# Sample attention in groups of four batches on the column quarters, and ScalarE's gates ahead of its state copies

## What is computed

```python
z = rmsnorm(x) @ w_in                                  # xr | gr | q | k | v | indexer ... | ga | gb
xc = causal_conv(xr)                                   # width 4
r, i = sigmoid(xc @ w_rg_a + b_a), sigmoid(xc @ w_rg_x + b_x)   # block diagonal
h[t] = a[t] * h[t-1] + sqrt(1 - a[t]**2) * i * xc      # a = exp(c * r * log_sigmoid(lam)); scan over positions
branch_a = (h * gelu(gr)) @ w_rnn_out
# sample rows: 8 batches, each with 256 past keys and values in two pages of a cache, and 4 new ones
p = softmax(mask(q @ k.T + bias)); o = p @ v           # 8 heads, mask from the indexer's top 65 keys
```

## Time and profile before

| | us |
|---|---|
| median of 3 runs | 1099.66 (1098.62 to 1100.06) |
| profiled execution, its own time | 1099.85 |
| span of the profiled execution | 1098.1 |
| PE busy | 1041.8 (95%) |
| DVE busy | 473.7 (43%) |
| ACT busy | 405.0 (37%) |
| POOL busy | 429.9 (39%) |

### The profile page before, as it was taken

The page is one execution under the profiler, slowest core; times in us unless marked ns, Lnnn a source line. Parts: engine busy times, 40 slices in busy tenths (PEclk is TensorE's granted clock), DMA queues, the critical chain, the costliest instruction groups (busy, mean ns, idle before and its releaser), DMA issues.

```text
span 1098.1 us, 19161 instructions
## 1 busy us (share of the span) xinstructions
PE 1041.8 (95%) x7847; PEld 978.8 (89%) x7847; DVE 473.7 (43%) x715; ACT 405.0 (37%) x690; POOL 429.9 (39%) x259
## 2 busy tenths in 40 slices
PE   4889999999997999999999899999999999999897
PEld 4777997777786889989999899999999999999797
DVE  2326899489988335323343413222100222212553
ACT  5424233556564434432332622222112222222534
POOL 2614432143435554534452534343444434343540
PEclk9999999999998999999999999999999999999899
DMA  6643274343312133304351332322233332222402
GB/s 180 176 78 91 60 197 133 118 116 96 96 40 77 23 80 97 97 23 124 106 164 54 103 100 85 95 67 73 87 101 106 87 95 62 61 85 81 116 1 82
DMA packets 168749, 101.96 MB, mean 93 GB/s; under 512 B 12626, under 2 KB 160754, under 8 KB 168418
## 3 DMA queue, kind: packets, MB, share of 16 engines
q1 hardware_dynamic: 168674, 100.91, 32.6%
HBM read 93.26 MB, written 7.63 MB: 92 GB/s over the span
## 4 chain that ended last, share of the span: by engine, by line
PE 81%; DVE 10%; ACT 4%; DMA 2%; issue 1%; POOL 1%; SPq 1%; DVEq 0%; ACTq 0%; POOLq 0%
PE psD L1723 71%; DVE xc L1133 3%; PE psX L1678 2%; DMA wraw<-in_w_in 1%; DVE hs L1283 1%; PE held L1678 1%; PE psX L1988 1%; PE held L1876 1%; PE held L2012 1%; DVE hs L1265 1%; DVE ig L1277 1%; PE psX L1806 1%; DVE h_lo L1063 1%; DMA prm<-in_state_rglru_h 1%; ACT L615 1%
## 5 line engine op out<-in xcount | busy, mean ns | idle before, releaser
L1509 POOL TENSOR_TENSOR wlo<-wraw,whi 128x1024 fp32r<-128x1024 f32 (+4 forms) x165 | 362.6, 2200 | 601.1 <-ACT whi L606 601.0
L1723 PE MATMUL psD<-h_hi,whi 128*128 128x272 f32 (+1 forms) x1616 | 347.8, 297 | 14.2 <-DVE h_lo L1063 9.8
L1723 PE MATMUL psD<-h_hi,wlo 128*128 128x272 f32 (+1 forms) x1616 | 338.8, 291 | 0.0
L1723 PE MATMUL psD<-h_lo,whi 128*128 128x272 f32 (+1 forms) x1616 | 338.4, 291 | 0.0
L1723 PEld LDWEIGHTS psD<-h_hi,whi 128*128 128x128 f32 (+1 forms) x1616 | 257.4, 191 | 34.8 <-issue 23.0
L1723 PEld LDWEIGHTS psD<-h_lo,whi 128*128 128x128 f32 (+1 forms) x1616 | 258.2, 191 | 0.0
L606 ACT CAST whi<-wraw 128x1024 fp32r<-128x1024 f32 (+4 forms) x165 | 154.8, 939 | 276.9 <-PE psD L1723 250.1
L1723 PEld LDWEIGHTS psD<-h_hi,wlo 128*128 128x128 f32 (+1 forms) x1616 | 256.9, 192 | 0.0
L1723 PE MATMUL psD<-act_hi,whi 128*128 128x272 f32 x672 | 140.9, 291 | 0.0
L1723 PE MATMUL psD<-act_hi,wlo 128*128 128x272 f32 x672 | 139.1, 288 | 0.0
L1723 PE MATMUL psD<-act_lo,whi 128*128 128x272 f32 x672 | 138.6, 288 | 0.0
(11 more groups left out here) (262 smaller groups left out, 942.2 us busy)
## 6 DMA issues: line engine op xcount, KB each, us to landing
wraw<-in_w_in SPq DMA_DIRECT2D x48, 512.0 KB, 4.6
wraw<-in_w_ffn_gate SPq DMA_DIRECT2D x22, 512.0 KB, 3.8
wraw<-in_w_ffn_up SPq DMA_DIRECT2D x22, 512.0 KB, 3.8
wraw<-in_w_ffn_down SPq DMA_DIRECT2D x16, 384.0 KB, 3.4
wraw<-in_w_ffn_down SPq DMA_DIRECT2D x16, 320.0 KB, 3.1
kpg<-in_cache_k SPq DMA_DIRECT2D x16, 256.0 KB, 3.0
kpg<-in_cache_v SPq DMA_DIRECT2D x16, 256.0 KB, 3.4
wraw<-in_w_rnn_out SPq DMA_DIRECT2D x8, 512.0 KB, 5.0
```

What stands on the lines that cost most here:

```text
L1509: g_.tensor_tensor(wlo[:, s, 0:rc, 0:cc], wraw[:, s, 0:rc, 0:cc], whi[:, s, 0:rc, 0:cc].bitcast(F32), ALU.subtract).then_inc(w_lo, 1)
L1723: ins = te.matmul(psD[0:cc, b0 + half, 0:HT], w[:, s, c, 0:cc], m[:, k0 + c, HT * half:HT * (half + 1)], start=(part == 0 and c == 0 and w ...
```

## The change

Four edits:
1. Past keys: four buffers `kts` in place of two. `past_logits(g4)` takes batches 4g to 4g+3 together, for each of the four contraction chunks one matmul on each column quarter in turn. PE's order: turns 0 to 3 between the halves of units 15 and 16, then logits of group 0 and turn 4 inside unit 17, turns 5 and 6, the five `vout` jobs, turn 7, logits of group 1.
2. Past values: four buffers `vpg` (the two of `kpg`, one over `kts[0]`, one over `qbd`). `past_values(g)` takes four batches together, group 0 in chunk 0 and group 1 behind gate sums (2, 1).
3. SP: value pages of batches 2 and 3 wait for both groups of logits, those of batches 4 to 7 for the first group of values; unit loads 25 and 26 come behind the first wait, 27 to 38 behind the eight page loads that follow the second.
4. ACT: in chunk c, `gates(c)` comes ahead of `final_states(c-1)`.

```diff
@@ buffers @@
+    kts = [place(f"kts{i}", [P, HP, PAST], F32, "act_lo", at) for i, at in enumerate((17920, 22016, 4096, 8192))]
+    vpg = kpg + [place("vpg2", [P, NPG, ATT], F32, "kts0"), place("vpg3", [P, NPG, ATT], F32, "qbd")]
@@ SP @@
                 job_read(sp, ("kts", NB - 2 + b, 1))
-                pages(kpg[b], "cache_v", b, kpg_in[b])
+                pages(vpg[b], "cache_v", b, vpg_in[b])
...
+            sp.wait_ge(slogit_q, 2)
+            for b in (2, 3):
+                pages(vpg[b], "cache_v", b, vpg_in[b])
             load(25)
             load(26)
-            for b in range(2, NB):
-                load(25 + b)
-                sp.wait_ge(spv_b, b - 1)
-                pages(kpg[b % 2], "cache_v", b, kpg_in[b % 2])
-            for n in range(33, 39):
+            sp.wait_ge(spv_q, 1)
+            for b in range(4, NB):
+                pages(vpg[b - 4], "cache_v", b, vpg_in[b - 4])
+            for n in range(27, 39):
                 load(n)
@@ ACT @@
-                    if b >= 2 and g == 0:
-                        act.wait_ge(slogit_b, b - 1)
+                    if b >= 4 and g == 0:
+                        act.wait_ge(slogit_q, 1)
...
             for c in range(DC):
+                gates(c)
                 if c >= 1:
                     final_states(c - 1)
-                gates(c)
                 if c == 0:
                     sample_turned()
@@ PE @@
-                job_read(pe, ("kts", q, 0))
-                job_read(pe, ("kts", q, 1))
+                job_read(pe, ("kts", 4 * g4 + 3, 0))
+                job_read(pe, ("kts", 4 * g4 + 3, 1))
                 for m in range(HP):
+                    for r in range(4):
+                        rows = slice(NS * r, NS * r + NS)
+                        ins = te.matmul(psX[2 + g4][rows, 0:PAST], qbd[:, m, 4 * g4 + r, :], kts[r][:, m, :],
+                                        start=(m == 0), stop=(m == HP - 1), tile_position=(0, NS * r))
+                ins.then_inc(slogit_q, 1)
...
+            def first_logits():
+                past_logits(0)
+                past_turn(4)
             run_around(U["v"] + 2, k_rows_last)
-            past_step(1)
-            run_around(U["v"] + 3, lambda: past_step(2))
-            past_step(3)
-            run_around(U["xr"], lambda: past_step(4))
-            past_step(5)
-            past_step(6)
+            past_turn(1)
+            run_around(U["v"] + 3, lambda: past_turn(2))
+            past_turn(3)
+            run_around(U["xr"], first_logits)
+            past_turn(5)
+            past_turn(6)
...
+            def past_values(g):
+                for r in range(4):
+                    pe.wait_ge(vpg_in[r], 16 * NPG * (g + 1))
                 for k in range(NPG):
+                    for r in range(4):
+                        rows = slice(NS * r, NS * (r + 1))
+                        ins = te.matmul(psX[2 + g][rows, :], pts[:, k, g, rows], vpg[r][:, k, :], start=False,
+                                        stop=(k == NPG - 1), tile_position=(0, NS * r))
+                ins.then_inc(spv_q, 1)
...
-                if 2 * c - 1 < NB:
-                    past_values(2 * c - 1)
+                if c == 2:
+                    past_values(1)
                 if c + 1 < DC:
                     run(n + 1)
-                if 2 * c < NB:
-                    past_values(2 * c)
```

More of the change, by code:

```diff
@@ L247, in hybrid_decoder_step @@
     kpg = [place(f"kpg{i}", [P, NPG, ATT], F32, "act_hi", 17408 + 4096 * i) for i in range(2)]
-    kts = [place(f"kts{i}", [P, HP, PAST], F32, "act_lo", 17920 + 4096 * i) for i in range(2)]
+    kts = [place(f"kts{i}", [P, HP, PAST], F32, "act_lo", at) for i, at in enumerate((17920, 22016, 4096, 8192))]
     pts = place("pts", [P, NPG, 2, P], F32, "act_lo", 12032)
@@ L310, in hybrid_decoder_step @@
         kpg_in, th_in, p_in, x_back = sems("kpg_in", 2), sems("th_in", 2), sem("p_in"), sem("x_back")
+        vpg_in = sems("vpg_in", 4)
         lines_saved, x_saved = sem("lines_saved"), sem("x_kept")
@@ L322, in hybrid_decoder_step @@
         topk_ok, topk_s_ok, mask_ok = sem("topk_ok"), sem("topk_s_ok"), sem("mask_ok")
-        qbd_ok, slogit_b, sexp_ok, sp_ok = sem("qbd_ok"), sem("slogit_b"), sem("sexp_ok"), sem("sp_ok")
-        spv_b, own_ok, so_hi = sem("spv_b"), sem("own_ok"), sem("so_hi")
+        qbd_ok, slogit_q, sexp_ok, sp_ok = sem("qbd_ok"), sem("slogit_q"), sem("sexp_ok"), sem("sp_ok")
+        spv_q, own_ok, so_hi = sem("spv_q"), sem("own_ok"), sem("so_hi")
         lru_a, lru_v, bd_zero, xe_ok, tap0 = sem("lru_a"), sem("lru_v"), sem("bd_zero"), sem("xe_ok"), sem("tap0")
@@ L706, in past_keys @@
                     got_job(act, ("kts", b, g))
-                    if b >= 2 and g == 0:
-                        act.wait_ge(slogit_b, b - 1)
-                    dst = kts[b % 2][:, :, PG * g:PG * (g + 1)]
+                    if b >= 4 and g == 0:
+                        act.wait_ge(slogit_q, 1)
+                    dst = kts[b % 4][:, :, PG * g:PG * (g + 1)]
                     src = bank(("kts", b, g))[:].rearrange("p (m s) -> p m s", s=PG)
@@ L827, in y_upper @@
                 act.wait_ge(yt_ok, c + 1)
+                if c == 6:
+                    act.wait_ge(spv_q, 2)
                 sc.copy(act_hi[:, c, :], hmul[c % 2][:]).then_inc(y_hi, 1)
@@ L1219, in _ @@
             conv_taps(0)
-            dve.wait_ge(slogit_b, NB)
+            dve.wait_ge(slogit_q, 2)
             dve.wait_ge(bias_in, 16 * 2 * NB // 2 * NJ)
@@ L1242, in sample_own @@
             def sample_own():
-                dve.wait_ge(spv_b, NB)
+                dve.wait_ge(spv_q, 2)
                 head = stat[:, 32:32 + NH].unsqueeze(2).broadcast_to([P, NH, HD])
@@ L1522, in y_lower @@
                 if c == 5:
-                    pool.wait_ge(spv_b, NB)
+                    pool.wait_ge(spv_q, 2)
                 g_.tensor_tensor(act_lo[:, c, :], hmul[c % 2][:], act_hi[:, c, :].bitcast(F32), ALU.subtract)\
@@ L1861, in past_turn, with past_logits @@
                     end_job(ins)
-            def past_logits(q):
-                if q == 0:
+            def past_logits(g4):
+                if g4 == 0:
                     pe.wait_ge(qbd_ok, 2 * HP)
@@ L1870, in past_logits @@
                                       start=(m == 0), stop=(m == HP - 1))
-                job_read(pe, ("kts", q, 0))
-                job_read(pe, ("kts", q, 1))
-                rows = slice(NS * (q % 4), NS * (q % 4) + NS)
-                out = psX[2 + q // 4]
+                job_read(pe, ("kts", 4 * g4 + 3, 0))
+                job_read(pe, ("kts", 4 * g4 + 3, 1))
                 for m in range(HP):
-                    ins = te.matmul(out[rows, 0:PAST], qbd[:, m, q, :], kts[q % 2][:, m, :], start=(m == 0),
-                              stop=(m == HP - 1), tile_position=(0, NS * (q % 4)))
-                ins.then_inc(slogit_b, 1)
+                    for r in range(4):
[3 more added lines that the diff above has]
+                ins.then_inc(slogit_q, 1)
             def k_rows_first():
@@ L1892, in k_rows_last @@
                 past_turn(0)
-            def past_step(q):
-                past_turn(q)
-                past_logits(q - 1)
+            def first_logits():
+                past_logits(0)
+                past_turn(4)
             run_around(U["v"] + 2, k_rows_last)
-            past_step(1)
-            run_around(U["v"] + 3, lambda: past_step(2))
-            past_step(3)
-            run_around(U["xr"], lambda: past_step(4))
-            past_step(5)
-            past_step(6)
+            past_turn(1)
[4 more added lines that the diff above has]
+            past_turn(6)
             all_read(pe, "v", HP)
@@ L1907, in _ @@
                 rows_out("vout", vT, t)
-            past_step(7)
-            past_logits(7)
+            past_turn(7)
+            past_logits(1)
             def gate_sums(c, g):
@@ L1924, in new_values @@
                 te.matmul(psX[2 + g][:], ptn[:, g, :], vtok_s[:], start=True, stop=False)
[L1926 to L1930, removed]
+            def past_values(g):
+                for r in range(4):
+                    pe.wait_ge(vpg_in[r], 16 * NPG * (g + 1))
                 for k in range(NPG):
-                    ins = te.matmul(psX[2 + g][rows, :], pts[:, k, g, rows], kpg[q % 2][:, k, :], start=False,
-                                    stop=(k == NPG - 1), tile_position=(0, NS * r))
-                ins.then_inc(spv_b, 1)
+                    for r in range(4):
[3 more added lines that the diff above has]
+                ins.then_inc(spv_q, 1)
             def sample_gather():
```

## The result

| | before | changed |
|---|---|---|
| median, us | 1099.74 (1098.62 to 1100.06, 4 runs) | 1117.20 (1117.06 to 1118.15, 4 runs) |
| ratio to before, 95% interval | | 1.0158 [1.0142, 1.0174] |
| profiled execution / its span, us | 1099.85 / 1098.1 | 1117.29 / 1115.6 |
| granted PE clock, mean of the span | 0.981 | 0.963 |

The change costs 17.5 us; 11.6 were forecast. Direction and mechanism hold, one term was too small. In the changed kernel the lines of DVE, ACT and PE stand six, four and six further down: the recurrence starts at line 1270 (1264 before), the taps are line 1139, the last state copy 827, the gate sums 1925, the logits 1882, the values 1939.

The account below looks back on a forecast made before the run. PE was taken to bound the past-keys stage, DVE with ACT the recurrent loop. Terms -6 + 3.0 + 14.6 = +11.6 on 1099.85 gave 1111.4 us (chance 0.57); range 1094 to 1119, the forecast's own 1106 to 1117.

Parts of the forecast that it names:

- The term that decides: Recurrent loop: state copies behind all five tanh delay line 1264; +3.0 us in chunk 1, +14.6 in chunks 2 to 6.
- Its size in chunks 2 to 6: Loop: five intervals of 21.57 us at PE's slow clock, 107.9 in place of 93.3, so +14.6 us.
- the first rival: Loop: PE stays at full clock, intervals of 19.98 us, +3.6 in sum, 1103.5 us; chance 0.14.
- POOL's part up to the taps' end: Loop: all three POOL subtractions lie ahead of the last tap; taps take 7.49 us, done 13.7 us into the recurrence.
- The first stage: Past keys: grouped logits end near 195 us in place of 201.6; gain taken as 6 us, bounds 3 and 10.7.
- the 10.7 us spared: Past-keys logits: PE work falls from 14.7 to 4.0 us; the upper bound of the gain.
- Values "nothing": Past values in the loop: grouping four batches gains 0 us, bounds 0 and -1, as DVE and ACT set the loop.
- Cover: DVE's busy time: Past values in the loop: PE's saved time is hidden behind DVE's work, so 0 us.
- SP and chunk 7: SP's 6 us of page-load issue stay hidden, 0 us; chunk 7 of the loop 0 us, bounds -1 and +3.
- Behind the loop: After the recurrent loop: the tail stays as before, 0 us.
- The signs named ahead: Loop and logits: line 1264 waits some 4 us for `stO`, starts 21.6 apart, slow PE clock, 32 records about 2 us.

Follow-up runs that it names:

- The old order: Changed kernel with ACT's state copies again ahead of the gates, groups of four kept: 1095.97 us, 0.9965 of before.
- the split: Changed kernel with the state copies between the three tanh on the first gate sums and the two on the second: 1091.97 us, 0.9926 of before.
- the sums together: Changed kernel with both gate sums of a chunk together between the halves of a unit: 1092.93 us, 0.9933 of before.
- The idle products: Changed kernel with unread matmuls added on PE ahead of gate sums (c, 0) in chunks 2 to 6: 1107.65 us, 1.0063 of before.
- one rounding later: Changed kernel with the second rounding of a chunk moved behind the next chunk's state copies: 1105.52 us, 1.0038 of before.

## Why the prediction was right or wrong

- **The term that decides, its mechanism.** Right. The old order takes all of the loss away, the split and the sums together each do too, and chunk 1, priced from rows alone, came out at +3.0.
- **Its size in chunks 2 to 6.** Wrong by 3.6 us: 111.51 instead of 5 x 21.57 = 107.9. The step that failed is the distance between the two gate sums, taken as 5.55 us from the one row behind a wait of 2.58 us. PE now waits 4.0 to 6.0 us, and in chunks 2 to 6 the distances are 6.08, 6.80, 5.71, 6.64 and 5.61, on average 6.17. That is 0.62 us a chunk, 3.1 of the 3.6. The rest is in the taps' end (13.8 us into the recurrence, against 13.7) and in the tanh and copies. The prediction said that PE would wait longer than in the row it took, and left the price as it was. The rows don't show that a longer wait by itself makes the distance longer: 5.61 stands behind 6.01 us and 6.80 behind 3.97. What they show is that the one row was the smallest of six. The idle products take 10.3 us of slow clock out of the five intervals.
- **The interval at full clock**, the first rival's 19.98: the idle products give 20.24. The time is 1107.65, not 1103.5: the five intervals are 1.3 us of that, and chunk 7, where the clock falls (19.95 against 17.92), is 2.0.
- **POOL's part up to the taps' end.** Right: three operations of POOL ahead of the last tap, 13.8 us; with one under the reciprocal, 11.7. But the first of them met the product (line 1279) and not the taps.
- **The first stage.** -5.5 (5.9 from the top-k's end) against -6. The group 1.93 us (2.0), turn 6 at 186.50 (186.0), logits ended at 196.1 (195), of which turn 6 at slow clock is about 0.9.
  "PE's new waits here can slow the unit that follows" is what came. The Trainium skill (TensorEngine Tiling (Array Packing), PSUM Bottleneck) says that the PSUM copy may become the bottleneck. This trace agrees only in part: the new wait, 2.58 us, is for ACT's copies out of PSUM, but they take 1.06 us (from 185.78); ahead of them ACT had the tile's copies, the tap and a rounding, from 183.14 on. Of the two measures of the overlap the row's held: 4 x 1.84 / 1.93 = 3.8 times, where the Trainium skill (TensorE: Matmul & The Clock Gate, Measured speedup vs the span model) has 3.07 for four row tiles and 2.38 for three column tiles.
  Eight batches were priced at 8 x 1.84 = 14.7 us, but the last two already took 2.81 together. That makes the 10.7 us spared, which was only a bound, 9.8; the sum does not use it.
- **Values "nothing".** Right in the changed kernel as the time of the groups goes, and half an answer. The step "Cover: DVE's busy time" looked at the time of the batches, not at what they did for PE's clock. With the new order alone and the batches left in, an interval is 20.2 us; with the groups it is 21.7 to 23.0. So the groups' price in the loop is of the size of their gain ahead of it. The sum held that price only because it took the slow clock in all five chunks, and it stood under the order, not under the values where it belongs.
- **SP and chunk 7.** SP's 6 us of issue show nowhere: ACT waits for no weight load between 200 and 380 us of the span. Chunk 7 is +0.3, inside its bounds.
- **Behind the loop**, 0 was forecast and 1.5 us came. No run was made for it. It is of the size of what this stretch, with the same code, differs by between the kernels above (758.4 to 760.0 us), so whether the change has a part in it stays open.

The signs named ahead came: `stO` in place of `rq`, waits above 4 us, the clock at 0.50 behind PE's, 1.93 us for a group. The starts are 22.3 us apart on average instead of 21.6.

Not tried: a second buffer for `hs`, which would take away the wait on the state copies altogether, smaller roundings so that ACT's order could be finer, and both gate sums together in the old order, which would say how much of the 1092.93 us is theirs alone.

## What to carry to other kernels

A signal is as late as the latest input of anything that stands ahead of it on its engine. Before an order is turned, list for each instruction that moves ahead what it waits for, and how that stands in the other engine's queue; if only some of a helper's inputs are early, split the helper (here 25.2 us between moving it whole and moving it by half). Price work that is taken off a waiting PE by the clock too: in this loop the two "free" batches a chunk, put back under the new order, made an interval 1.6 to 2.8 us shorter. And when an engine comes free of one wait, look at what its long operations meet next. Here one POOL operation moved from under DVE's taps to under its reciprocal was worth 12.8 us (1091.97 to 1079.18), more than the groups were in any order.

## What was not expected of the hardware

- Added matmuls made the kernel faster: 28 idle products in each of four chunks and 16 in a fifth, 1117.20 to 1107.65 us. Behind the waits of these chunks the granted clock stayed at 1.00 (windows 238.6 to 242.7 and 258.8 to 262.9).
- After waits of 4 to 6 us the same half unit with its sums took between 5.6 and 6.8 us, with no order by the length of the wait in these rows: 6.08 behind 6.00 us, 6.80 behind 3.97. The length of a slow stretch is to be taken as a range. Nor does the wait's length alone say whether the clock falls: behind 1.85 us (one rounding later, chunk 3) it fell to 0.70 in the mean of the stretch (259.0 to 264.6), and the sums were 5.60 us apart; behind 3.06 us (changed kernel, chunk 7) it stayed at 1.00, and they were 4.04 apart.
- DVE's reciprocal takes 3.70 us whether a POOL subtraction runs beside it or not, and the subtraction takes 2.38; beside the taps it took up to 2.85, and the three taps 7.49 instead of 4.48. The product ahead of the taps takes 0.74 us alone and 2.95 beside a subtraction.
- Four batches of logits on four quarters, batch by batch, took 4.57 us, though no neighbouring pair changed its quarter within a batch; 7.4 had been expected. The 2.81 us of two batches together had shown it.
